# The first conditioning vectors of a two-layer diffusion backbone: three groups on VectorE and one on TensorE, in place of two and two

## What is computed

```python
def modulate(h, mod, j):
    return h * (1.0 + mod[..., 3 * j + 1, :, :]) + mod[..., 3 * j, :, :]

def half_ffn(h, mod, j, w, g, b, alpha):
    y = swiglu(modulate(h, mod, j), *w)
    return layer_norm(alpha * h + 0.5 * gate(mod, j) * y, g, b)
```

## Time and profile before

| | |
|---|---|
| median of 3 runs | 2110.05 us (2109.68 to 2113.74) |
| the profiled execution | 2107.69 us |
| its span, first to last instruction | 2106.0 us |
| PE busy in the span | 1973.3 us (94%) |
| DVE busy | 1260.3 us (60%) |
| ACT busy | 639.8 us (30%) |
| first instruction of the first ffn on PE | 58.97 us |

### The profile page before, as it was taken

How to read it: one execution, slowest core, us unless ns; L and a number is a source line. 1 busy time by engine, 2 the same in 40 slices (tenths; PEclk the granted TensorE clock), 3 DMA queues, 4 the chain that set the end, 5 groups by cost and what they waited for, 6 DMA issues and landing times.

```text
span 2106.0 us, 23288 instructions
## 1 busy us (share of the span) xinstructions
PE 1973.3 (94%) x8800; PEld 1501.7 (71%) x8800; DVE 1260.3 (60%) x2151; ACT 639.8 (30%) x1057; POOL 304.5 (14%) x298
## 2 busy tenths in 40 slices
PE   8999999889999988799999997999999799889996
PEld 8788878745454455378887875888778457779996
DVE  3676776542682655577768438774677535355454
ACT  2322242222342432232224223222333230424442
POOL 0000001150000000600000123000034535130003
PEclk9999999998998999899999998999999899989998
DMA  8255536322241000334553333453234635214442
GB/s 347 81 203 196 192 142 165 120 91 103 76 167 75 1 0 5 135 136 184 199 199 126 120 129 126 166 207 146 101 112 183 246 120 190 80 41 156 166 174 103
DMA packets 43954, 290.04 MB, mean 138 GB/s; under 512 B 13916, under 2 KB 19676, under 8 KB 27232
## 3 DMA queue, kind: packets, MB, share of 16 engines
q1 hardware_dynamic: 34336, 270.08, 34.7%
q10 hardware_dynamic: 9536, 18.88, 2.4%
HBM read 272.16 MB, written 16.78 MB: 137 GB/s over the span
## 4 chain that ended last, share of the span: by engine, by line
PE 82%; DVE 9%; ACT 3%; DMA 3%; POOL 1%; issue 1%; ACTq 0%; SPq 0%; POOLq 0%; DVEq 0%
PE bank L582 12%; PE bank L587 12%; PE bank L584 12%; PE bank L647 6%; PE bank L640 6%; PE bank L644 6%; PE bank L741 3%; PE bank L725 3%; PE bank L914 2%; PE bank L689 2%; PE bank L738 2%; PE bank L823 1%; PE bank L679 1%; PE bank L911 1%; PE bank L547 1%
## 5 line engine op out<-in xcount | busy, mean ns | idle before, releaser
L1581 DVE CUSTOM_DVE_ANT_0 L<-slot 128x1024 f32<-128x1024 f32 x272 | 336.8, 1238 | 79.7 <-DMA slot<-in_ada_dram 72.5
L1088 ACT ACTIVATE w_hi<-slot 128x1024 fp32r<-128x1024 f32 x176 | 186.3, 1061 | 570.9 <-PE bank L587 558.7
L1620 DVE TENSOR_TENSOR w_lo<-slot,w_hi 128x1024 fp32r<-128x1024 f32 x176 | 217.1, 1236 | 225.8 <-ACT w_hi L1088 219.1
L582 PE MATMUL bank<-m_hi,w_hi 128*128 128x512 f32 (+1 forms) x1344 | 296.7, 363 | 1.2 <-ACT w_hi L1088 1.2
L584 PE MATMUL bank<-m_lo,w_hi 128*128 128x512 f32 (+1 forms) x1344 | 296.1, 363 | 0.0
L587 PE MATMUL bank<-m_hi,w_lo 128*128 128x512 f32 (+1 forms) x1344 | 296.1, 362 | 0.0
L582 PEld LDWEIGHTS bank<-m_hi,w_hi 128*128 128x128 f32 x1344 | 232.3, 189 | 41.8 <-ACT w_hi L1088 2.7
L584 PEld LDWEIGHTS bank<-m_lo,w_hi 128*128 128x128 f32 x1344 | 232.6, 189 | 39.3
L587 PEld LDWEIGHTS bank<-m_hi,w_lo 128*128 128x128 f32 x1344 | 232.6, 189 | 39.2
L1738 DVE TENSOR_TENSOR down_lo<-slot,down_hi 128x1408 fp32r<-128x1408 f32 x64 | 108.8, 1710 | 137.4 <-ACT down_hi L1136 137.1
L644 PE MATMUL bank<-g_lo,down_hi 128*128 128x512 f32 (+1 forms) x704 | 152.9, 365 | 0.1
(11 more groups left out here) (335 smaller groups left out, 2645.3 us busy)
## 6 DMA issues: line engine op xcount, KB each, us to landing
slot<-in_gateup_dram SPq DMA_DIRECT2D x44, 2048.0 KB, 7.8
slot<-in_ada_dram SPq DMA_DIRECT2D x34, 2048.0 KB, 7.8
slot<-in_down_dram SPq DMA_DIRECT2D x32, 1408.0 KB, 6.1
slot<-in_ev_in_dram SPq DMA_DIRECT2D x4, 2048.0 KB, 9.6
slot<-in_od_in_dram SPq DMA_DIRECT2D x4, 2048.0 KB, 10.0
R<-s_ops SPq DMA_DIRECT2D x16, 512.0 KB, 5.9
s_tables<-slot ACTq DMA_DIRECT2D x8, 768.0 KB, 3.3
R<-s_tables SPq DMA_DIRECT2D x8, 768.0 KB, 6.8
```

The lines of the kernel that those rows point to most:

```text
L582: nc.tensor.matmul(bank[j][:, c0:T], w_hi[:, off, c, :], m_hi[:, c, c0:T], start=(c == 0), stop=False)
L1088: nc.scalar.activation(w_hi[:, off, :, :].rearrange("p a b -> p (a b)"), slots[b][:, (2 * (f % 2) + off) * D:(2 * (f % 2) + off + 1) * D], ...
L1581: ins = nc.vector.tensor_tensor_reduce(out=junk, in0=slots[k][:, t * D:(t + 1) * D], in1=csilu[s_], scale=1.0, scalar=0.0, op0=ALU.mult, o ...
L1620: nc.vector.tensor_tensor(w_lo[b][:, t, :, :].rearrange("p a b -> p (a b)"), slots[b][:, t * D:(t + 1) * D], w_hi[:, off, :, :].bitcast(F3 ...
```

## The change

Group 2 goes to DVE and group 3 stays with PE. The two early loads change places: the first one now brings group 3, the second one group 2. PE and ACT do four turns in place of eight. DVE, after groups 0 and 1, waits for both early loads and does the eight products of group 2 from the second half of R, in a new `early_modulation`; then come the rests of the first weights, then the bias of group 3 from PE's bank, then the fold. Bytes, sizes and the places of the DMAs in SP's queue are as before.

```diff
-            sp.dma_start(ada_early[0], i["ada"][2]).then_inc(sem("ada_early_in"), 16)
+            sp.dma_start(ada_early[0], i["ada"][3]).then_inc(sem("ada_early_in"), 16)
...
-            sp.dma_start(ada_early[1], i["ada"][3]).then_inc(sem("ada_early_in"), 16)
+            sp.dma_start(ada_early[1], i["ada"][2]).then_inc(sem("ada_early_in"), 16)
...
                 turn(0)
-                for t in range(2 * 4):
-                    if t + 1 < 2 * 4:
+                for t in range(4):
+                    if t + 1 < 4:
                         turn(t + 1)
...
-                for t in range(2 * 4):
+                for t in range(4):
                     act.wait_ge(sem("ada_turned"), t + 1)
...
+            def mods_early(g_, sums_):
+
+                mcount[0] += 1
+                flat = lambda buf: buf[:, :, :, :].rearrange("p a b c -> p (a b c)")[:, 8 * g_:8 * g_ + 8]
+                nc.vector.tensor_tensor(flat(mods), sums_, flat(modb), ALU.add).then_inc(sem("mods_ready"), 1)
+
+            def early_modulation(src):
+
+                dve.wait_ge(sem("ada_early_in"), 32)
+                dve.wait_ge(sem("mods_ready"), mcount[0])
+                for j in range(8):
+                    t, s_ = j // 2, j % 2
+                    nc.vector.tensor_tensor_reduce(out=L[:, 2 * T:4 * T], in0=src[:, t * D:(t + 1) * D], in1=csilu[s_], scale=1.0, scalar=0.0,
+                                                   op0=ALU.mult, op1=ALU.add, accum_out=ada_sum[:, t, s_:s_ + 1]).then_inc(sem("ada_early_done"), 1)
+                    dve.wait_ge(sem("ada_early_done"), j + 1)
+                mods_early(2, ada_sum[:, :, :].rearrange("p a b -> p (a b)"))
+
             dve.wait_ge(sem("csilu_ready"), 2)
             for g_ in range(2):
                 for half in range(2):
                     modulation(1 + g_ % 2, half)
+            early_modulation(ada_early[1])
...
-            for g_ in range(2, 4):
-                dve.wait_ge(sem("ada_summed"), 4 * (g_ - 1))
-                mcount[0] += 1
-                flat = lambda buf: buf[:, :, :, :].rearrange("p a b c -> p (a b c)")[:, 8 * g_:8 * g_ + 8]
-                nc.vector.tensor_tensor(flat(mods), banks[4 + g_][:, 0:8], flat(modb), ALU.add).then_inc(sem("mods_ready"), 1)
+            dve.wait_ge(sem("ada_summed"), 4)
+            mods_early(3, banks[6][:, 0:8])
             fold(0)
```

More of the change, by code:

```diff
@@ L530, in turn @@
                 def turn(t):
-                    if t % 4 == 0:
-                        pe.wait_ge(sem("ada_early_in"), 16 * (t // 4 + 1))
+                    if t == 0:
+                        pe.wait_ge(sem("ada_early_in"), 16)
                     if t >= 2:
@@ L537, in turn @@
                         last = nc.tensor.transpose(banks[2 * (t % 2) + c // 4][:, (c % 4) * P:(c % 4 + 1) * P],
-                                                   ada_early[t // 4][:, (t % 4) * D + c * P:(t % 4) * D + (c + 1) * P], ident[:, :])
+                                                   ada_early[0][:, t * D + c * P:t * D + (c + 1) * P], ident[:, :])
                     last.then_inc(sem("ada_turned"), 1)
                 turn(0)
-                for t in range(2 * 4):
-                    if t + 1 < 2 * 4:
+                for t in range(4):
+                    if t + 1 < 4:
                         turn(t + 1)
@@ L546, in early_modulation @@
                     for c in range(KT):
-                        last = nc.tensor.matmul(banks[6 + t // 4][:, 2 * (t % 4):2 * (t % 4) + 2], ada_turned[:, t % 2, c, :], ccol[:, :, c],
+                        last = nc.tensor.matmul(banks[6][:, 2 * t:2 * t + 2], ada_turned[:, t % 2, c, :], ccol[:, :, c],
                                                 start=(c == 0), stop=(c == KT - 1))
```

## The result

The changed kernel took 2093.42 us (median of 10 runs, 2088.08 to 2100.55), the kernel before 2109.75 us beside it (10 runs, 2107.48 to 2113.74): ratio 0.9931, 95% interval 0.9914 to 0.9949. (A ratio is a kernel's time over that of the kernel before, run beside it; the interval stands behind it in brackets from here on.) That is 16.3 us faster on the medians, where 10.9 was forecast, and 2.1 us under the low end of the range. The profiled execution took 2094.51 us, its span is 2092.4.

The account below looks back on a forecast made before the run. The prediction took PE's work to bound the kernel (82% of the chain), its eight early turns delaying the ffn. A head 10.9 us shorter, with no cost for clock or loads, gave 2110.05 - 10.9, say 2099.1 us; range 2095.5 to 2103.5.

Parts of the forecast that it names:

- PE's side: PE's turns ahead of the ffn: four go, 20.06 us; group 3 ready at about 36.7, ACT at `w_hi` at 31.0.
- DVE's side: DVE ahead of the fold: eight products from 33.1, set by the second early load, 10.14 us, with bias addition to 43.4.
- The uncovered rests of the weights: DVE's rests of the first ffn weights, hidden before, now follow group 2: 2.36 us, from 43.4 to 45.8.
- The sum of the head: All ahead of the ffn: ACT's first modulated tile at 46.3 instead of 57.21, 10.9 us shorter.
- The loads: x lands at 38.1, 8.2 us ahead of need; ffn loads land by 47.4 to 59.8, at worst 0.8 us lost.
- Rival 3: Second early load lands late, delaying DVE's group 2 and the ffn; slower by over 0.2% from 48.1 on; chance 0.02.
- Rival 1: At the first down weights' load, 287.56 us: the head's gain is given back, time 2110; chance 0.05.
- Rival 2: PE's old work held the clock, so the first ffn tile runs slow and longer: 2.0 us, 2101.2; chance 0.05.
- the term of the clock: PE's clock at the first ffn tile: same lower level, no cost; bounds 1.0 us loss, 2.0 us gain.
- The start of the sum: Whole kernel: the median of three runs, 2110.05 us, from which the head's 10.9 us were taken.
- the range: Whole kernel: 2095.5 to 2103.5 us, from the clock's bounds, 2097.1 to 2100.1, and the scatter of earlier runs.

Follow-up runs that it names:

- no_swap: The changed kernel with the two early loads in their old order, so PE waits for the second: 2097.93 us, ratio 0.9944.
- pe_filler96: The changed kernel with 96 transposes more on PE behind group 3, waited for by nobody: 2093.51 us, ratio 0.9928.
- before_c: The kernel before, unchanged, run again for a fourth trace: 2107.80 us, ratio 1.0006.
- pe_filler: The changed kernel with 40 transposes more on PE in its pause ahead of the ffn, waited for by nobody: 2089.64 us, ratio 0.9908.

## Why the prediction was wrong, point by point

- **PE's side: right.** Four turns dropped, ACT free for `w_hi` at 31.13.
- **DVE's side: right.** The second early load set the start of its products (0.38 us of wait, 33.13), and they ran at the price of the earlier trace rows: 8 products and the addition from 33.13 to 43.36. The swap, costed at nothing because it changes nothing in the queue, is what lets PE begin at once: `no_swap` is 6.5 us later.
- **The uncovered rests of the weights: right.** They now stand on the chain, 2.27 us. The sum of the head was 10.9, measured 11.1.
- **The loads: right.** x and the slots of the ffn were never waited for in the head.
- **Rival 3** (the second load late) did not come: it landed at 33.1. But it now is on the chain, with the first, for 30 of the first 33 us; in `no_swap` PE stood behind it instead, at a cost of 6.5 us. **Rival 1** did not come either: the head's gain went through the down load and to the end.
- **Rival 2 and the term of the clock: wrong, and this is the step that failed.** I said "The level is the same, so I take no cost", and bounded the term by the first tile alone, 2.0 us to the good and 1.0 to the bad. That the tile still begins at the lower level is right. But the clock falls and rises again many times behind it, and the time behind the start was 4.3 us less (standard error 1.0) with the changed kernel, and 5.5 us less (0.6) with all kernels of four turns together against those with eight. In the traces the loss carries this. The term has to be taken over the whole span: it comes to 44.7 to 63.1 us here, in single executions, and I gave it the 4.4 us of one tile. That it would be some 4 us lower with the change no row of the kernel before says, and why it was stays open. That the term is large could be seen: the span's mean granted clock in the profile is 0.962, and the earlier trace rows showed a stretch of 6.5 us where the earlier trace rows had 4.4.
- **The start of the sum and the range.** The forecast went out from the median of three runs, 2110.05; the mean over 126 is 2107.9. Of the 6.6 us between the forecast of 2099.1 and the changed kernel's mean of 2092.5, these are 2.1, the head 0.2 and the time behind it 4.3. I took the scatter from the three runs (0.4 below, 3.7 above). With the profiled execution's 2.4 below, which the same sentence names, the low end would have been 2097.1 - 2.4 = 2094.7 and not 2095.5; the 2093.42 lie under that as well. The kernel before has a standard deviation of 3.4 us over 126 runs, the changed one 4.3 over 22. A head computed to 0.2 us stands on a tail that moves by 4.

By the Trainium skill's rule on pauses ("TensorE: Matmul & The Clock Gate", section "HAM oscillation — how this bites in real kernels") the pause would have cost time. The traces show no such cost: the first tile, up to the first matmul of the next one, took 12.6 to 13.6 us in three traces of the changed kernel and 13.2 to 13.5 in four of the kernel before, since it began at the lower level in both; and the time behind it went down, not up. In `pe_filler96`, where the pause was filled densely, the first tile took 11.2 us, as the rule has it.

## What to carry to other kernels

When two engines share out independent work ahead of a critical start, read each one's price per share from the trace, see when each is free, and divide so that both end together; what was hidden behind the slower one (here 2.36 us of weight rests) belongs in the new sum. Such a sum can be right to 0.2 us. Where PE alternates between dense and sparse stretches, the time at the lower clock can differ between executions by more than such a gain, so price a change from landmarks in the trace, compare times over dozens of runs, and split a difference into what lies ahead of a landmark and what lies behind it before explaining it.

## What the runs showed of the hardware

- 45 to 63 us of loss at the lower clock in executions of almost the same work: with it the span behind the ffn's start goes from 2037 to 2054 us, over a rest that is constant within 2.2 us in 15 traces.
- During PE's turns (transposes and products of two columns, each waiting for the other and for ACT's copies) the clock came up in eight of 18 traces, from about 20 us to 23 or 24 (26 in `before_c`), and in the other ten not at all, though PE is busy in nearly all of the 40 us of eight turns. During 96 transposes back to back it came up at about 41.5, 5 us after the first of them, and stayed up into the ffn. During the 40 of `pe_filler` it came up too, at 37.5, and was down again at the ffn's start, behind 7.88 us of idle PE.
- Fewer turns ahead of the ffn go with 5.5 us less behind its start (62 runs against 150), and in the traces with a smaller loss (49.7 against 57.2 us on the mean), most of it hundreds of us later. It is measured, and not explained.
